# Moving two thirds of a kernel's SBUF tensors by 64 bytes

## The reference

```python
for l in range(2):        # first_block
    rq, rk, rv, rg, cq, ck, cv, dq, dk, dv, gates = split(x @ w_in[l])
    o_a = retention(rq, rk, rv, rg); o_b = chunk_attention(cq, ck, cv, rel_bias)
    o_c = diff_attention(dq, dk, dv, lam)
    g = sigmoid(gates + b_merge[l])
    merged = g0 * (o_a @ w_branch_a[l]) + g1 * (o_b @ w_branch_b[l]) + g2 * (o_c @ w_branch_c[l])
    x = layer_norm(ALPHA * x + merged @ w_out[l], ln1_g[l], ln1_b[l])
    x = layer_norm(ALPHA * x + swiglu(x, w_ffn_in[l], w_ffn_out[l]), ln2_g[l], ln2_b[l])
for l in range(2):        # second_block, weights *_2
    x = layer_norm(ALPHA * x + 0.5 * swiglu(x, ffn1...), ln1)
    y = concat(short_conv, gmlp_spatial, nsa_attention)      # all from x @ w_in_2[l]
    x = layer_norm(ALPHA * x + y @ w_out_2[l], ln2)
    x = layer_norm(ALPHA * x + 0.5 * swiglu(x, ffn2...), ln3)
```

## The kernel before, in words

| tensor | first byte in the partition | start modulo 128 |
|---|---|---|
| raw, hl, cst | 384, 24960, 74112 | 0 |
| maskb | 82848 | 32 |
| xs, xt, o1, o2, gb, th, tm, rt, er, ai, et, mhalf | 83616, 91808, 108192, 124576, 132768, 140960, 145056, 155296, 159392, 169632, 170144, 178336 | 32 |
| small, stage, stage2, gn, zb | 178368, 183744, 184256, 185280, 187328 | 64 |
| q1, k1, sg, w2, qkv, v1 | 189408, 193504, 197600, 205792, 206304, 222688 | 96 |

## Time and profile before

### The profile page before, as it was taken

The page is one execution under the profiler, slowest core; times in us unless marked ns, Lnnn a source line. Parts: engine busy times, 40 slices in busy tenths (PEclk is TensorE's granted clock), DMA queues, the critical chain, the costliest instruction groups (busy, mean ns, idle before and its releaser), DMA issues.

```text
span 2026.5 us, 32504 instructions
## 1 busy us (share of the span) xinstructions
PE 2010.0 (99%) x14176; PEld 1835.6 (91%) x14176; DVE 1274.6 (63%) x1844; ACT 927.0 (46%) x1275; POOL 32.2 (2%) x56
## 2 busy tenths in 40 slices
PE   8999999999999999999999999999999999999998
PEld 7888999999887999999999989799999998979997
DVE  6566666555756665655665567765566556776555
ACT  4445444444545444544444454454444445445442
POOL 0000000000000000000000000000000000000000
PEclk9999999999999999999999999999999999999999
DMA  8544555666544555586556646458656664555663
GB/s 287 168 149 132 187 172 168 199 207 190 167 163 136 167 168 186 147 261 187 167 181 188 185 135 167 105 157 251 187 167 188 187 188 134 158 136 157 189 188 101
DMA packets 416133, 352.51 MB, mean 174 GB/s; under 512 B 28816, under 2 KB 361080, under 8 KB 415992
## 3 DMA queue, kind: packets, MB, share of 16 engines
q1 hardware_dynamic: 415992, 350.44, 57.3%
HBM read 349.36 MB, written 1.05 MB: 173 GB/s over the span
## 4 chain that ended last, share of the span: by engine, by line
PE 94%; DVE 3%; ACT 2%; issue 0%; DMA 0%; DVEq 0%; SPq 0%
PE ps L201 29%; PE ps L202 29%; PE ps L203 29%; PE ps L1446 2%; PE ps L1527 2%; PE ps L1565 1%; DVE hl L1990 1%; PE ps L1599 1%; ACT hl L1749 1%; DVE er L2157 0%; DVE small L2116 0%; ACT er L1841 0%; PE ps L1637 0%; DVE er L2114 0%; PE ps L1570 0%
## 5 line engine op out<-in xcount | busy, mean ns | idle before, releaser
L1990 DVE TENSOR_TENSOR hl<-raw,hl 128x1024 fp32r<-128x1024 f32 (+2 forms) x555 | 756.3, 1393 | 393.5 <-ACT hl L1749 392.5
L201 PE MATMUL ps<-xt,hl 128*128 128x256 f32 (+1 forms) x2672 | 753.5, 282 | 0.0
L202 PE MATMUL ps<-xt,hl 128*128 128x256 f32 (+1 forms) x2672 | 746.0, 279 | 0.0
L203 PE MATMUL ps<-xt,hl 128*128 128x256 f32 (+1 forms) x2672 | 745.5, 279 | 0.0
L1749 ACT ACTIVATE hl<-raw 128x2048 fp32r<-128x2048 f32 (+1 forms) x323 | 612.8, 1899 | 183.6 <-PE ps L203 169.4
L201 PEld LDWEIGHTS ps<-xt,hl 128*128 128x128 f32 (+1 forms) x2672 | 501.0, 187 | 4.7 <-issue 1.5
L202 PEld LDWEIGHTS ps<-xt,hl 128*128 128x128 f32 (+1 forms) x2672 | 500.9, 187 | 3.2
L203 PEld LDWEIGHTS ps<-xt,hl 128*128 128x128 f32 (+1 forms) x2672 | 500.8, 187 | 0.2
L201 PE MATMUL ps<-hl,o 128*128 128x512 f32 x656 | 261.9, 399 | 0.0
L203 PE MATMUL ps<-hl,o 128*128 128x512 f32 x656 | 259.4, 395 | 0.0
L202 PE MATMUL ps<-hl,o 128*128 128x512 f32 x656 | 259.4, 395 | 0.0
(11 more groups left out here) (202 smaller groups left out, 1605.8 us busy)
## 6 DMA issues: line engine op xcount, KB each, us to landing
raw<-in_w_in SPq DMA_DIRECT2D x83, 1024.0 KB, 5.1
raw<-in_w_ffn_in SPq DMA_DIRECT2D x88, 512.0 KB, 5.2
raw<-in_ffn_gate SPq DMA_DIRECT2D x88, 512.0 KB, 4.0
raw<-in_ffn_up SPq DMA_DIRECT2D x88, 512.0 KB, 5.3
raw<-in_ffn_down SPq DMA_DIRECT2D x44, 1024.0 KB, 5.0
raw<-in_w_ffn_out SPq DMA_DIRECT2D x22, 1024.0 KB, 5.0
raw<-in_w_out SPq DMA_DIRECT2D x12, 1024.0 KB, 5.1
raw<-in_w_branch_a SPq DMA_DIRECT2D x8, 1024.0 KB, 4.9
```

The lines of the kernel that those rows point to most:

```text
L201: e.matmul(out, l[0], r[0], start=start, stop=False)
L202: e.matmul(out, l[0], r[1], start=False, stop=False)
L203: return e.matmul(out, l[1], r[0], start=False, stop=stop)
L1990: e.tensor_tensor(lo[:, c], m["raw"][:, k % NRAW, 0:n][:, c], hi[:, c].bitcast(F), ALU.subtract).then_inc(s.low.up(("low", k), *([("low", ...
```

## The change

One more tensor, `apart`, of 16 fp32 elements (64 bytes) in each of the 128 partitions, is taken between `maskb` and `xs`. Nothing reads or writes it.

```diff
             "const": sb("cst", [128, NCONST]), "maskb": sb("maskb", [128, 3, 128], BF),
+            "apart": sb("apart", [128, 16]),
             "x": sb("xs", [128, 2, D]), "xt": sb("xt", [128, 2, 8, S], R),
```

## The result

The changed kernel takes 2056.86 us (median of 4 runs, 2056.29 to 2057.73) against 2027.85 us for the kernel before (4 runs beside it, 2027.23 to 2028.76): a ratio of 1.0142, 95% interval 1.0129 to 1.0155, so 29.0 us slower. The profiled span is 2055.3 us, against 2026.5.

What follows compares the result with a forecast made beforehand. The prediction took TensorE's matmul stream to bound the kernel. Zero for VectorE and ScalarE, loads, moving operand and DMA left the profiled 2028.55 us, as a median 2027.7 us, range 2024.4 to 2031.7.

Steps and rivals of the forecast that it cites:

- What bounds the kernel: Whole kernel: TensorE's matmul stream sets the time, 1804 us, 89% of the span; one per cent of its rate is 18 us.
- VectorE, ScalarE, weight loads, DMA, at zero: Vector and scalar instructions, weight loads and transfers on moved tensors: durations unchanged, each 0 us in the sum.
- TensorE, moving operand, at zero: The 8736 matmuls streaming a moved tensor: rate unchanged, 0 us, with bounds of 14.6 us either way.
- one of the signs by which the forecast said that it would be wrong: Starts inside an unbroken run of `t_part` matmuls having another distance than 116.7 ns.
- The two classes: Starts modulo 128 of fp32r moving operands: hl at 0, xt at 32, both streaming at 0.456 ns a column.
- Rival A: `t_part`, xt or o1 streaming past hl weights: TensorE reads moved rows slower, +14.6 us, 2042.3 us; chance 0.07.
- The 672 matmuls of the earlier trace: Matmuls loading xt while hl streams in 256 columns: their extra 1.67 ns may vanish or double, 1.1 us; taken as zero.
- Rival B: TensorE's stream: 64 bytes partly remove a collision, 14.6 us faster, 2013.1 us, at the far end 1964; chance 0.05.

Runs made afterwards that it cites:

- e3_all64: Kernel before with 64 bytes in front of raw, so every tensor from raw on, hl too, moves by 64 and all distances stay: 2027.23 us.
- e4_hl64: Kernel before with 64 bytes in front of raw and 64 behind hl: raw and hl move by 64, xs and all behind by 128; 2056.13 us.
- e6_xt64: Kernel before with 64 bytes in front of xt and 64 behind o2: xt, o1, o2 move by 64, gb and all behind by 128; 2056.21 us.
- e5_raw64: Kernel before with 64 bytes in front of raw and 64 behind it: raw moves by 64, hl and all behind by 128; 2027.49 us.
- e15_pair: Kernel before with low parts of the weights and of xt, o1 and o2 both set 64 bytes further from their high parts: 2033.40 us.

## Why the prediction was wrong

*What bounds the kernel* was right: the stream was the lever. The 29.0 us are 1.6% of the 1804 us that it summed, and nothing else moved by as much as 1 us.

*VectorE, ScalarE, weight loads, DMA, at zero:* right. Lines 2017 and 2192 took 693 and 692 ns against 691 and 693, line 1721 stayed at 379, a load of line 203 at 188, the output's DMA at 2.1 us to landing with 0% of the chain. TensorE's growth is the whole loss, and no wait took part.

*TensorE, moving operand, at zero: this step failed.* It put "equal rates at two classes stand nearest". Measured, the starts inside `t_part` stand 119.9 ns apart in the mean and no longer 116.7, 27.1 us on the matmuls with xt or o moving; it is one of the signs by which the forecast said that it would be wrong. The fault is in what was compared. The two classes, moving at 0 with stationary at 32 and the reverse, were taken as evidence that the start doesn't matter; they were two roles at one spacing of the same two tensors, and the 512-column stream of one was set against the 256-column stream of the other. What the rate goes by is the distance of the two operands modulo 256, and a shift of one tensor changes it for every matmul that pairs it with one that stays. Nor do rates per column carry over from 512 to 256 columns: at distance 0 they are 227.2 / 512 = 0.444 and 119.9 / 256 = 0.468 ns, so the two equal 0.456 were a coincidence. The pair that did compare like with like, 118.3 against 116.7 ns at 256 columns, showed the effect plainly: d = 224 against d = 32. It was priced and given 0.07 as a loss and 0.05 as a gain. The argument that a long row "runs through eight or more pieces of 128 bytes wherever it starts" speaks of one stream alone and says nothing of two that run beside each other.

*Rival A had the place and the dependence right:* something "that depends on how the two operands, read at the same time and in a fixed phase, lie to each other". e3_all64, e4_hl64 and e6_xt64 show the dependence; that it is a collision in SBUF isn't shown. Its size was off: 1.67 ns were taken from the only pair at hand, 3.1 were measured, 27.1 us on 8784 matmuls against the 14.6 given. Its sign said that the rows of 512 columns stay unchanged; they went from 233.2 to 234.2 ns, the other 2.2 us. The range, made from the forecast's own terms and leaving out 0.12 of the chance, ended at 2031.7, 25.2 us below the measured time.

*The 672 matmuls of the earlier trace rows* went from 118.3 to 117.8 ns, 0.2 us, inside the 1.1 us allowed.

*Rival B*, the faster side of the same dependence, exists: not at 64 bytes but at 160, with 32.1 us of gain.

A sentence of the Trainium skill bears on this. The page "SBUF — State Buffer", section "Who interferes with whom", gives TensorE two independent read ports, one for the moving operand and one for weight loads, and says that TensorE never waits on anyone. Towards the other engines the traces agree, by the 116.7 ns of e5_raw64 and the idle hole above. By "independent" one would expect no effect of how the two operands lie to each other; 64 bytes between them took the mean from 116.7 to 119.9 ns, and the measurement decides.

## What to carry to other kernels

Where TensorE is the bound and its matmuls stream slower than their columns at the granted clock, look at the distance, modulo 256 bytes, between the moving and the stationary tensor: any tensor added, resized or removed between them shifts it, and a change of size elsewhere can be blamed for, or credited with, what the shift did. In this kernel that was from -1.6% (1996.59 us) to +1.4% (2056.86 us). Try a few pads of 32 to 224 bytes between the two before and after a change of layout, and compare versions of a kernel at equal distance. A placement is a term of the sum like a wait: "no instruction changed" isn't a reason for zero.

## What the runs showed of the hardware

- An fp32r stream with a weight load for every matmul takes 113.5 to 120.0 ns for 256 columns and 227.2 to 234.2 ns for 512, at the same granted clock of 0.999, depending on the operands' distance modulo 256. Distance 0, with 119.9 ns among the worst for 256 columns, is the best for 512 (227.2 ns). Why the two differ isn't known. That the distance matters and not the start is shown by moving tensors at 64 bytes; that the period is 256 bytes, by the pads of 128, 256 and 512.
- Once a stretch has settled, its rate hardly moves: in 72 of the 74 stretches of 48 and more in the changed kernel, all means of twelve distances after the first dozen lie within 0.6 ns of one another. They lie all over the span, beside whatever VectorE, ScalarE and DMA do there. With the pads of 96 and 192 bytes these means vary more.
- At some distances a stretch settles at one of two or three rates, 113.3 or 117.8 ns with the pad of 160; what selects it stays open, and with it whether 1996.59 us can still be lowered by placing xt, o1 and o2 each by itself. That wasn't tried.
- Open too is which pair of reads it is: e15_pair's 117.85 ns lies between what the two simple readings give, so a matmul's rate depends on more than one of its neighbours.
